# Two blocks of a transformer on one core: in the second block, products over 64 rows run in pairs on the two halves of the TensorE array, and the first queries are turned between two halves of a projection

## What is computed

```
u = rmsnorm(h) @ w_in                        # q (8 heads of 64), k, v (2 groups of 64),
                                             # qi (16 index heads of 64), ki (64), wi (16), conv, pool
dots = einsum('thd,sd->ths', qi, ki)         # index heads: 16 x (256 x 256), contraction over 64
idx  = einsum('ths,th->ts', relu(dots), wi)  # causal; the 64 largest of each row are kept
s    = q_head @ k_group.T * 64**-0.5         # 8 heads, contraction over 64, kept keys only
out  = softmax(s) @ v_group
mix  = [out, conformer_conv(u_conv), multiscale_pool(u_pool)] @ w_out
```

## Time and profile before

| what | value |
|---|---|
| median of three runs | 1879.25 us |
| the profiled execution's own time | 1880.8 us |
| its span, first to last instruction | 1879.0 us |
| TensorE products busy | 1854.1 us (99%), 15946 instructions |
| TensorE weight loads busy | 1840.6 us (98%) |
| VectorE busy | 1342.0 us (71%) |
| ScalarE busy | 1001.7 us (53%) |
| GpSimd busy | 127.1 us (7%) |
| mean granted TensorE clock | 0.996 of full |
| chain that ended last | TensorE 91%, VectorE 5%, ScalarE 3% |

### The profile page before, as it was taken

The page is one execution under the profiler, slowest core; times in us unless marked ns, Lnnn a source line. Parts: engine busy times, 40 slices in busy tenths (PEclk is TensorE's granted clock), DMA queues, the critical chain, the costliest instruction groups (busy, mean ns, idle before and its releaser), DMA issues.

```text
span 1879.0 us, 36714 instructions
## 1 busy us (share of the span) xinstructions
PE 1854.1 (99%) x15946; PEld 1840.6 (98%) x15946; DVE 1342.0 (71%) x1661; ACT 1001.7 (53%) x1251; POOL 127.1 (7%) x110
## 2 busy tenths in 40 slices
PE   8999999999999999999999999999999999899998
PEld 8999999999999999999999999999999999899998
DVE  7755788785558755788776556888866688787566
ACT  6444555564447544546564445867543467664434
POOL 1000000000000000000000000263000005600000
PEclk9999999999999999999999999999999999999999
DMA  8556555565554655555556555523565644047552
GB/s 268 205 188 202 170 151 170 167 204 188 193 202 163 225 193 189 182 159 173 178 170 202 187 195 172 180 91 95 182 214 189 204 128 154 29 159 244 194 189 68
DMA packets 246531, 329.55 MB, mean 175 GB/s; under 512 B 6246, under 2 KB 218788, under 8 KB 246372
## 3 DMA queue, kind: packets, MB, share of 16 engines
q1 hardware_dynamic: 246018, 326.79, 52.8%
q0 software_dynamic: 96, 0.26, 0.1%
q10 hardware_dynamic: 258, 0.16, 0.0%
HBM read 326.14 MB, written 1.05 MB: 174 GB/s over the span
## 4 chain that ended last, share of the span: by engine, by line
PE 91%; DVE 5%; ACT 3%; issue 1%; DMA 0%; DVEq 0%; ACTq 0%
PE work L2121 21%; PE work L2122 21%; PE work L2123 21%; PE acc L2121 9%; PE acc L2122 9%; PE acc L2123 9%; ACT w_hi L802 1%; DVE w_lo L1355 1%; PE work L2307 1%; DVE fa L1818 1%; PE acc L2223 1%; DVE fa L1894 0%; ACT cs L1088 0%; DVE small L1891 0%; DVE ra L1368 0%
## 5 line engine op out<-in xcount | busy, mean ns | idle before, releaser
L1355 DVE TENSOR_TENSOR w_lo<-raw,w_hi 128x2048 fp32r<-128x2048 f32 (+1 forms) x308 | 681.8, 2215 | 91.2 <-ACT w_hi L802 91.0
L2121 PE MATMUL work<-x_rows,w_hi 128*128 128x256 f32 x2560 | 710.0, 277 | 0.9 <-DVE x_rows L1389 0.7
L2122 PE MATMUL work<-x_rows,w_hi 128*128 128x256 f32 x2560 | 705.9, 276 | 0.0
L2123 PE MATMUL work<-x_rows,w_lo 128*128 128x256 f32 x2560 | 705.8, 276 | 0.0
L802 ACT ACTIVATE w_hi<-raw 128x2048 fp32r<-128x2048 f32 (+2 forms) x313 | 579.0, 1854 | 163.4 <-PE work L2123 68.9
L2121 PEld LDWEIGHTS work<-x_rows,w_hi 128*128 128x128 f32 x2560 | 482.0, 188 | 2.0 <-DVE x_rows L1389 1.2
L2122 PEld LDWEIGHTS work<-x_rows,w_hi 128*128 128x128 f32 x2560 | 481.9, 188 | 0.3
L2123 PEld LDWEIGHTS work<-x_rows,w_lo 128*128 128x128 f32 x2560 | 481.8, 188 | 0.0
L2121 PE MATMUL acc<-ra,w_hi 128*128 128x256 f32 x1352 | 372.4, 275 | 0.0
L2122 PE MATMUL acc<-ra,w_hi 128*128 128x256 f32 x1352 | 372.0, 275 | 0.0
L2123 PE MATMUL acc<-ra,w_lo 128*128 128x256 f32 x1352 | 372.0, 275 | 0.0
(11 more groups left out here) (322 smaller groups left out, 2245.3 us busy)
## 6 DMA issues: line engine op xcount, KB each, us to landing
raw<-in_ffn_w_gu_dram SPq DMA_DIRECT2D x88, 1024.0 KB, 5.1
raw<-in_w_in_dram SPq DMA_DIRECT2D x52, 1024.0 KB, 5.4
raw<-in_ffn_w_down_dram SPq DMA_DIRECT2D x44, 1024.0 KB, 5.0
raw<-in_w_up_dram SPq DMA_DIRECT2D x32, 1024.0 KB, 5.5
raw<-in_w_down_dram SPq DMA_DIRECT2D x32, 1024.0 KB, 4.9
raw<-in_w_mla_out_dram SPq DMA_DIRECT2D x8, 1024.0 KB, 5.4
raw<-in_w_o_dram SPq DMA_DIRECT2D x8, 1024.0 KB, 5.4
raw<-in_w_ple_gate_dram SPq DMA_DIRECT2D x8, 1024.0 KB, 5.2
```

What stands on the lines that cost most here:

```text
L1355: v.tensor_tensor(w_lo[:, s, 0:n], raw[:, r, 0:n], w_hi[:, s, 0:n].bitcast(F32), ALU.subtract).then_inc(lo_done.sem, 1)
L2121: pe.matmul(dst, ah, bh, start=start and i == 0, stop=False, skip_group_check=not group)
L2122: pe.matmul(dst, ah, bl, start=False, stop=False, skip_group_check=not group)
L2123: last = pe.matmul(dst, al, bh, start=False, stop=stop and i == len(pairs) - 1, skip_group_check=not group)
```

## The change

Four edits, all in the second block.

1. `side_by_side` is new: for each of the three parts of a float32 product it issues one TensorE product on rows 0 to 63 and one on rows 64 to 127 of the array (tile_position), each with 64 rows of queries and of keys, into two PSUM banks.
2. `dots`: the 12 late products go through it, tile by tile (bank 1 takes the heads on rows 0 to 63, bank 2 those on rows 64 to 127); both banks are waited for at the start and told ready together at the end. `weighted` takes the heads in the matching order.
3. `scores` makes two heads at a time (hd and hd + 1, 12 products, two units, told ready together) and is called at heads 0, 2 and 4 instead of 0 to 5. The list of units follows.
4. The first queries are turned between the two halves of `by_token` for ("q", 1), and VectorE's `queries_lo(0)` moves from r = 7 to r = 6, ahead of the rotation of the second queries.

```diff
-    names += [("q", 0), "kt", ("q", 1), ("qt", 0), ("sc", 0), ("sc", 1), ("qt", 1)]
+    names += [("q", 0), "kt", ("qt", 0), ("q", 1), ("sc", 0), ("sc", 1), ("qt", 1)]
     for hd in range(HEADS):
-        names += [("pt", hd)] + ([("sc", hd + 2)] if hd + 2 < HEADS else []) + ([("out", hd - 1)] if hd else [])
+        names += [("pt", hd)] + ([("sc", hd + 2), ("sc", hd + 3)] if hd % 2 == 0 and hd + 2 < HEADS else []) + ([("out", hd - 1)] if hd else [])
...
                     if r == 6:
+                        queries_lo(0)
                         rope_unit(("q", 1), "q1")
-                    if r == 7:
-                        queries_lo(0)
...
+            def side_by_side(dsts, queries, keys):
+
+                for i, (a, b) in enumerate(((0, 0), (0, 1), (1, 0))):
+                    for half in range(2):
+                        rows = slice(64 * half, 64 * half + 64)
+                        last = pe.matmul(dsts[half], queries[a][rows], keys[half][b][rows], start=i == 0, stop=i == 2,
+                                         tile_position=(64 * half, 0), skip_group_check=True)
+                return last
...
+                    if c:
+                        pe.wait_ge(*dot_taken.at(here, 3 * c - 2))
+                    for tile in range(2):
+                        last = side_by_side([acc[:, 1 + half, tile * T:tile * T + T] for half in range(2)],
+                                            (qih[:, c % 2, tile, P:T], qil[:, c % 2, tile, P:T]),
+                                            [(keys[:, 0, 2, :], keys[:, 1, 2, :]) for keys in (ka, kb)])
+                    last.then_inc(dot_ready.sem, 2)
...
-                by_token(Q2 + 1, ("q", 1))
-                pe.wait_ge(*unit_taken.at(here, U2["q", 0]))
-                turned(("qt", 0), tm[:, 0, :, :])
+
+                def first_queries():
+                    pe.wait_ge(*unit_taken.at(here, U2["q", 0]))
+                    turned(("qt", 0), tm[:, 0, :, :])
+
+                by_token(Q2 + 1, ("q", 1), first_queries)
...
                 def scores(hd):
-                    u = U2["sc", hd]
-                    free(here, u)
-                    keys = (ka, kb)[hd % 2]
+
+                    units = [U2["sc", hd + half] for half in range(2)]
+                    for u in units:
+                        free(here, u)
                     for tb, at in ((0, 0), (1, P)):
                         n, queries = P * (tb + 1), slice(tb * P, tb * P + P)
-                        last = product(bank(u)[:, at:at + n],
-                                       [((qh[:, hd // 2, queries], ql[:, hd // 2, queries]),
-                                         (keys[:, 0, hd // 4, 0:n], keys[:, 1, hd // 4, 0:n]))])
-                    last.then_inc(unit_ready.sem, 1)
+                        last = side_by_side([bank(u)[:, at:at + n] for u in units],
+                                            (qh[:, hd // 2, queries], ql[:, hd // 2, queries]),
+                                            [(keys[:, 0, hd // 4, 0:n], keys[:, 1, hd // 4, 0:n]) for keys in (ka, kb)])
+                    last.then_inc(unit_ready.sem, 2)
...
                     probs(hd)
-                    if hd + 2 < HEADS:
+                    if hd % 2 == 0 and hd + 2 < HEADS:
```

More of the change, by code:

```diff
@@ L1812, in weighted @@
                         for g in range(512 // n):
-                            hd = INDEX_HEADS[c] + (2 * i if i < 2 else 0) + g
+                            hd = INDEX_HEADS[c] + (2 * g + i if i < 2 else g)
                             src = acc[:, 1 + i, g * n:g * n + n]
@@ L2509, in token_half, with by_token @@
                                                                 columns(w, k * 256, 256)) for k in range(KD)])
-                def by_token(c, unit):
+                def by_token(c, unit, between=None):
                     free(here, U2[unit])
@@ L2515, in by_token @@
                     for tb in range(TB):
+                        if tb and between is not None:
+                            between()
                         last = token_half(c, unit, tb, w)
@@ L2529, in dots @@
                     pe.wait_ge(*unit_taken.at(here, U2["qit", c]))
[L2530 to L2540, removed]
+                    if c:
[5 more added lines that the diff above has]
+                    last.then_inc(dot_ready.sem, 2)
+                    if c:
+                        pe.wait_ge(*dot_taken.at(here, 3 * c - 1))
+                    for g in range(4):
+                        keys = (ka, kb)[g % 2]
+                        last = product(acc[:, 3, g * P:g * P + P],
+                                       [((qih[:, c % 2, g // 2, 0:P], qil[:, c % 2, g // 2, 0:P]),
+                                         (keys[:, 0, 2, 0:P], keys[:, 1, 2, 0:P]))])
+                    last.then_inc(dot_ready.sem, 1)
                 project(here, G2_IN, U2["g"])
@@ L2623, in _ @@
                 scores(0)
-                scores(1)
                 pe.wait_ge(*unit_taken.at(here, U2["q", 1]))
```

## The result

| what | before | after |
|---|---|---|
| median | 1879.2 us (6 runs, 1878.78 to 1881.45) | 1886.74 us (6 runs, 1883.94 to 1889.83) |
| the profiled execution | 1880.8 us, span 1879.0 | 1889.83 us, span 1888.0 |
| mean granted clock | 0.996 | 0.987 |

The ratio is 1.0034 with a 95% interval of 1.0024 to 1.0043 (of the two medians alone, 1.0040). The kernel became slower, outside the range of the forecast. The six executions of after stand in two groups, 1883.94 to 1884.54 and 1888.93 to 1889.83, and the profiled one is the longest of the upper group, so costs read from its trace are on the high side.

The account below looks back on a forecast made before the run. TensorE's products and weight loads were taken to bound the kernel, with small idle time and low clock at the first queries. Terms -2.4 - 3.0 - 1.05 - 0.2 + 1.0 = -5.65 us gave 1873.6 us, range 1871.5 to 1879.2.

Parts of the forecast that it names:

- the sum: Whole kernel: both attention stretches and index heads gain, less changes between paired and whole products, -5.65 us in all.
- the rival that has one: Heads 0 to 2: new waits drop the clock until 1280, +2.9 us per layer, +5.8; slower kernel, chance 0.08.
- cheap pairs: Index and score products: two 64-row halves load and run side by side, 0.07 us per product with ends.
- the two tails: Attention stretches to their last transposes: gains of 2.4 us in layer 0 and 3.0 in layer 1.
- First queries sooner, layer 0: Layer 0: the 2.15 us wait goes, low clock costing 1.7 us goes, head 0's probabilities come 3.2 us ahead.
- Layer 1: First queries in layer 1: waits of 1 us mid-projection and 1.1 at the end; head 0's probabilities 3.9 us ahead.
- What the pairs of scores give back: Heads 0 to 3, layer 0: new waits of 1.3 and 1.8 us leave 1.4 or 0.9 of 3.2 us gained.
- change of kind: Between whole and paired products: the array runs empty, 0.16 us each, 32 changes; bounds 0 and 0.35.
- Index heads: Late products of `dots`: 1.05 us saved in layer 0, 0.2 in layer 1; 1.0 paid for six exposed changes.
- Pairs in series: Paired products: both halves' loads share one path, pairs save nothing; -4.4 or -1.5 us in all; chance 0.31.
- nothing from turning: First queries: the wait only moves into the projection, leaving -1 to -2 us (1878); chance 0.06.

Follow-up runs that it names:

- x12: After, with 12, 6, 5, 8 and 4 zero products ahead of five waits at heads 0 and 4 and the score pairs: 1878.79 us, ratio 0.9992.
- x1: Before with only the sooner turning of the first queries (edit 4), scores and index products unchanged: 1877.52 us, ratio 0.9986.
- x14: After, with 12 zero products ahead of head 0's exp wait alone: 1884.57 us, ratio 1.0023.
- x13: Before, with 18 zero products in layer 0 and 38 in layer 1 ahead of the wait for the first queries: 1879.27 us, ratio 0.9990.
- x9: Before with the sooner turning and the index pairs, plus 14 zero products ahead of head 0's exp wait: 1877.47 us, ratio 0.9981.
- x8: Before with the sooner turning alone, plus 14 zero products ahead of head 0's exp wait: 1876.43 us, ratio 0.9978.
- x15: After, with 6 and 5 zero products ahead of the second pool product and head 0's output alone: 1880.73 us, ratio 1.0005.
- x3: After, with 12, 11 and 14 zero products ahead of head 0's exp wait, second pool product and head 0's output: 1880.25 us, ratio 1.0003.
- x6: After, with 12, 11, 14, 9 and 5 zero products ahead of waits at heads 0 and 4 and the last score pair: 1879.82 us, ratio 0.9992.

## Why the prediction was wrong

**Two steps failed.** The first is the clock: the sum has no term for a fall behind head 0, and the rival that has one was priced and weighed too low. It said: the clock falls in the new waits, stays down to 1280, + 2.9 us per layer, 0.08. The fall is there, from 1271.0; but the clock came back only at 1291.4, and the price is 5.35 and 5.50 us per layer in the traces (x12 against after), and about 4 per layer by the ratios. The rival's condition, that on cheap pairs the kernel becomes slower once the clock costs more than 5.65, is met either way (10.85, or 7.9). No row of the prediction supports an end at 1280; the falls in the earlier trace rows are 4 and 6.6 us long. The 7.48 of 9.0 us busy at full clock was taken as the mark of a density that keeps the clock. x1 and x14 show that it does not decide by itself: layer 0 of x1 keeps the clock with 3.63 and 3.91 busy of 5 us, x14 loses it with 4.30 and 3.42.

The second is the gain, - 2.4 and - 3.0 us in the two tails: at full clock the whole change gains 2.4 us, not 5.65 (x12). The forecast had head 0's output at 1275.2; at full clock it stands at 1276.06 (0.23 of that because the stretch starts later), because the second pool product waits for head 0's split and the output for head 3's mask. Of x12:

```profile
1276.06 0.30 PE L2120 MATMUL work<-vp,ra 128*128 128x64 f32 x1 [0.65 <-DVE fa L1461]
```

The 3.25 us of missing gain and the 7.9 to 10.85 us of clock make 11 to 14 us; the forecast missed by 1886.74 - 1873.6 = 13.1.

Point by point, by the forecast's own steps:

- *First queries sooner, layer 0.* Right: the wait of 2.15 us went to 0, VectorE masked head 0 at 1267.64 (forecast 1267.3), ScalarE's exp began at 1268.88 (1268.4), and the probabilities came 2.5 us ahead (3.2). The low clock there had cost 0.69 us (x13), where I had 1.7.
- *Layer 1.* The waits are 1.53 us in the middle and 0.89 at the end (forecast 1 and 1.1). Head 0's probabilities came 73.12 us after the start of the stretch, 75.67 before: 2.6 us ahead, not 3.9. What the step brought was the clock (x13).
- *What the pairs of scores give back.* The new waits stand where they were placed, before the second pool product and head 0's output, 0.68 and 0.51 us instead of 1.3 and 1.8. They were short, and the loss came all the same.
- *The tails, 2.4 and 3.0 us.* At full clock the whole change, index pairs in it, gains 1.35 and 1.03 (x12), and against before at full clock (x13) nothing. The pairs of scores were booked as a gain behind head 0 and are a loss of about 0.9 us per layer there.
- *Cheap pairs.* Right: 0.12 per two products, loads too. A change of kind shows as 0.21 between 1212.50 and 1212.71, where two pairs stand 0.12 apart, and the next distances are longer too. Over both changes around `dots(1)`, the last projection product stands 1.40 us ahead of the third early product (1221.12 to 1222.52), 1.73 before (1220.88 to 1222.61). So of the 6 x 0.12 = 0.72 us that the pairs save 0.33 is left, and a change costs about 0.2; I had 0.16.
- *Index heads.* I had -1.05 and -0.2, with +1.0 for changes of kind. The runs show -0.30 and -0.08 (x9 against x8), about the same net.
- *Pairs in series* did not come, and *nothing from turning* neither (x1: 0.9986).

The rows on VectorE and ScalarE for the first of these points, of after:

```profile
1267.64 0.56 DVE L1461 SCALAR_TENSOR_TENSOR fa<-work,fa 128x384 f32<-128x384 f32 x1
```

```profile
1268.88 0.40 ACT L1187 ACTIVATE fa<-fa,small 128x128 f32<-128x128 f32 x1 [0.43 <-DVE small L1465]
```

and of TensorE in layer 1:

```profile
1605.41 0.66 PE L2315 MATMUL work<-consts,fa 128*128 128x128 f32 x4 [1.53 <-ACT fa L1070]
...
1611.14 0.67 PE L2586 MATMUL acc<-fa,vrow 128*128 128x256 f32 x2 [0.89 <-DVE ra L1368]
...
1617.62 0.52 PE L2315 MATMUL work<-consts,fa 128*128 128x128 f32 x3 [2.17 <-ACT fa L1187]
```

and before:

```profile
1615.71 0.49 PE L2307 MATMUL work<-consts,fa 128*128 128x128 f32 x3
```

A passage on this mechanism exists: the Trainium skill (TensorE: Matmul & The Clock Gate, A second HAM failure mode: psum-queue depth-cycling) describes a kernel in which short idle times between groups of matmuls, from cycling through PSUM banks, made the clock go up and down. The trace agrees in part: x14's clock falls right behind a bank wait of 1.01 us, but it falls once per layer and stays down, and in after it fell ahead of the bank waits of 0.68 and 0.51 us. I had not weighed it.

## What to carry to other kernels

Where TensorE is busy nearly all the time, look at the granted clock before the waits: a rearrangement that adds two half-microsecond waits to a place where TensorE already waits cost 4 to 5 us per layer here through the clock, and the busy share does not show it. Ask of a change of bank order which short waits it puts close together, and price the rival on the clock by the longest stretch that a fall might last, not by the length of the falls already in the trace. A quick test is to fill the suspected waits with zero products: if the kernel gets faster by doing more, it was the clock. Take more than one trace, or lean on the medians: the same code lost the clock at one place in one execution and kept it there in another (after and x15).

The best that ran is the turning alone, with 14 zero products ahead of head 0's exp wait: 1876.43 us, ratio 0.9978 [0.9969, 0.9987]. It beats both kernels; from the other versions without the score pairs of heads 2 to 7 the intervals don't separate it.

## What the hardware showed that was not expected

- The clock stays at its lower level with TensorE recorded busy almost without a pause: from 1276.5 to 1291.4 in after, 14.90 of 14.90 us, and in layer 1 from 1624.0 to 1639.6. Before, it came back within 4 and 7 us. What makes the difference is open. One thing goes with it in all ten profiled executions with a fall in these stretches: the ten falls of 10 us and more hold 15 to 27 products of 64 columns (the head outputs) each, the nine of under 7 us hold none, apart from one in x15 with five. No run took those products out of a fall, so that they keep the clock down is not shown.
- Products with a zero matrix hold the clock where they fill a wait (x3, x6, x12, x13).
- Which short waits matter doesn't follow from their length or their sum. Behind the exp wait of 1.62 us the clock stays up in layer 0 of x1 and x15 and falls in after; with that wait filled, 1.01 us behind it is enough in x14.
- Two products on 64 rows, loads included, start together and cost one distance of 0.12 us; at half clock products of 64, 128 and 256 columns all stand about 0.21 to 0.22 apart.
